# Scan stage of a hybrid decoder step: the sample states advanced once ahead of the 32 steps, and the rotation products made by cosine and by sine over both parts at a time

## The reference

```
bu_re, bu_im = einsum(u, bb_re), einsum(u, bb_im)
h(l) = a * h(l-1) + bu(l)          # complex, a = mag * (cos + i sin), over the 256 prompt tokens from zero
h    = a * h0 + bu                 # for the 8 sample rows: one step from a carried state h0
y    = einsum(c_re, h_re) - einsum(c_im, h_im) + d * u
```

## Time and profile before

| | |
|---|---|
| median of 3 runs | 1678.98 us (1677.73 to 1684.87) |
| the profiled execution | 1680.68 us, its span 1678.9 us |
| PE busy | 1550.0 us (92%) |
| DVE busy | 735.7 us (44%) |
| ACT busy | 330.2 us (20%) |
| POOL busy | 215.4 us (13%) |
| mean granted clock of TensorE | 0.964 |

### The profile page before, as it was taken

How to read it: one execution, slowest core, us unless ns; L and a number is a source line. 1 busy time by engine, 2 the same in 40 slices (tenths; PEclk the granted TensorE clock), 3 DMA queues, 4 the chain that set the end, 5 groups by cost and what they waited for, 6 DMA issues and landing times. The chain is left out here.

```text
span 1678.9 us, 21005 instructions
## 1 busy us (share of the span) xinstructions
PE 1550.0 (92%) x8121; PEld 1093.6 (65%) x8121; DVE 735.7 (44%) x1989; ACT 330.2 (20%) x873; POOL 215.4 (13%) x304
## 2 busy tenths in 40 slices
PE   7999998998989888999999799859999999999996
PEld 5888886776767666888887378735454454455444
DVE  3546429999974743000334300151343343343344
ACT  3111010111113222110112100133123222222214
POOL 1111026656630000110000000120000000000000
PEclk9999998999999889999999899969999999999998
DMA  9743443333342547444576876305999999999971
GB/s 277 225 149 110 151 151 104 106 118 125 99 135 87 158 138 256 151 150 135 175 258 231 299 211 247 153 2 217 404 405 383 404 402 389 394 403 401 382 323 52
DMA packets 203393, 376.19 MB, mean 224 GB/s; under 512 B 25011, under 2 KB 158431, under 8 KB 178450
## 3 DMA queue, kind: packets, MB, share of 16 engines
q1 hardware_dynamic: 198634, 370.62, 60.5%
q10 hardware_dynamic: 4664, 4.28, 0.7%
HBM read 363.44 MB, written 11.54 MB: 223 GB/s over the span
## 5 line engine op out<-in xcount | busy, mean ns | idle before, releaser
L932 PE MATMUL ps<-ring,M 128*128 128x256 f32 x1024 | 246.1, 399 | 1.6 <-ACT M L945 1.6
L932 PEld LDWEIGHTS ps<-ring,M 128*128 128x128 f32 x1024 | 201.1, 200 | 42.3 <-issue 14.6
L2463 PE MATMUL ps<-ring,M 128*64 128x512 f32 x1024 | 223.3, 594 | 0.3 <-ACT M L2552 0.3
L645 PE MATMUL ps<-X,ring 128*128 128x264 f32 x896 | 205.1, 390 | 0.0
L645 PEld LDWEIGHTS ps<-X,ring 128*128 128x128 f32 x896 | 171.0, 192 | 29.2 <-issue 0.4
L2463 PEld LDWEIGHTS ps<-ring,M 128*64 128x64 f32 x1024 | 72.1, 137 | 137.8 <-issue 137.0
L315 PE MATMUL ps<-SH,ring 128*128 128x264 f32 x512 | 116.1, 391 | 6.4 <-PEq L1512 6.4
L1861 PE MATMUL ps<-X,ring 128*128 128x264 f32 x512 | 117.7, 387 | 1.6 <-PEq L1565 1.6
L315 PE MATMUL ps<-X,ring 128*128 128x264 f32 x512 | 114.2, 387 | 1.0 <-PEq L1687 1.0
L2507 PE MATMUL ps<-SH,M 128*64 128x512 f32 x512 | 113.4, 595 | 1.3 <-DVE XT L2680 1.3
L315 PEld LDWEIGHTS ps<-SH,ring 128*128 128x128 f32 x512 | 98.7, 193 | 23.8 <-issue 6.8
(11 more groups left out here) (462 smaller groups left out, 1842.8 us busy)
## 6 DMA issues: line engine op xcount, KB each, us to landing
SH<-in_moe_w_down SPq DMA_DIRECT2D x32, 2048.0 KB, 12.0
ring<-in_moe_w_gate SPq DMA_DIRECT2D x64, 1024.0 KB, 11.6
ring<-in_moe_w_up SPq DMA_DIRECT2D x64, 1024.0 KB, 13.8
ring<-in_w_in SPq DMA_DIRECT2D x14, 2048.0 KB, 8.2
ring<-in_xa_wk SPq DMA_DIRECT2D x8, 2048.0 KB, 9.3
ring<-in_xa_wv SPq DMA_DIRECT2D x8, 2048.0 KB, 9.1
ring<-in_w_out SPq DMA_DIRECT2D x8, 2048.0 KB, 8.6
ring<-in_xa_wq SPq DMA_DIRECT2D x8, 2048.0 KB, 8.6
```

Source lines behind the costliest of these rows:

```text
L645: mm = nc.tensor.matmul(ps[:, n % 4, 0:T], w[:, d, o * P:(o + 1) * P], xn[:, d, :], start=(d == 0), stop=(d == KB - 1))
L932: mm = nc.tensor.matmul(ps[:, kv_bank(s), a * 256:(a + 1) * 256], memT[:, k, a * P:(a + 1) * P], w[:, k, :], start=(k == 0), stop=(k == KB ...
L2463: mm = nc.tensor.matmul(ps[64 * e:64 * e + 64, 0, :], xg[:, p % 3, k, e, :], gate_up_unit(e, half)[:, :, k % 8, :], start=(k == 0), stop=( ...
```

## The change

DVE's program of the scan stage is changed, nothing else. Ahead of the step loop four instructions compute the carried states times `a` for all 32 steps at once, into `carried` (and a helper `carried_b`) in a free part of `work`. In a step one instruction then adds the input to `carried` in place of four that computed the product and the sum. The products with the cosine are made over the real and imaginary parts in one instruction of 128x512 (the cosine repeated by a stride of zero), and those with the sine likewise, ahead of the scans and behind them. The sums and differences stay as they were, and read other places of `pr`.

```diff
+        carried, carried_b = (work[:, 2112 + 512 * i:2624 + 512 * i].rearrange("p (i b t) -> p i b t", i=2, b=TS)
+                              for i in range(2))
...
+                by_cos, by_sin = pr[:, 0:2], pr[:, 2:4]
+                every_b = lambda j, n: s5p[:, j, :].unsqueeze(1).to_broadcast([P, n, 32])
+                both = lambda x: x.rearrange("p i b t -> p (i b) t")
+                tt(both(carried), both(s5h[:, :, :, :]), every_b(AR, 16), ALU.mult)
+                tt(carried_b[:, 0], s5h[:, 1], every_b(NAI, 8), ALU.mult)
+                st(tt(carried_b[:, 1], s5h[:, 0], every_b(AI, 8), ALU.mult))
+                st(tt(both(carried), both(carried), both(carried_b), ALU.add))
                 for t in range(NT):
...
-                    tt(pr[:, 0], br[:, 0:TP], cos, ALU.mult)
-                    tt(pr[:, 1], bi[:, 0:TP], sin, ALU.mult)
-                    tt(pr[:, 2], bi[:, 0:TP], cos, ALU.mult)
-                    stt(hr[:, TP:T], s5h[:, 0, :, t], sc(AR), br[:, TP:T], ALU.mult, ALU.add)
-                    stt(hi[:, TP:T], s5h[:, 1, :, t], sc(AR), bi[:, TP:T], ALU.mult, ALU.add)
-                    tt(pr[:, 3], br[:, 0:TP], sin, ALU.mult).then_inc(bu_taken.sem, bu_taken.up())
+                    tt(by_cos, bu[:, :, 0:TP], cos, ALU.mult)
+                    tt(by_sin, bu[:, :, 0:TP], sin, ALU.mult)
+                    tt(hb[:, t % 4, :, TP:T], carried[:, :, :, t], bu[:, :, TP:T], ALU.add).then_inc(
+                        bu_taken.sem, bu_taken.up())
                     dve.wait_ge(bu_taken.sem, bu_taken.at(t + 1))
-                    tt(gin[:, 0], pr[:, 0], pr[:, 1], ALU.add)
-                    stt(hr[:, TP:T], s5h[:, 1, :, t], sc(NAI), hr[:, TP:T], ALU.mult, ALU.add)
-                    stt(hi[:, TP:T], s5h[:, 0, :, t], sc(AI), hi[:, TP:T], ALU.mult, ALU.add)
-                    st(tt(gin[:, 1], pr[:, 2], pr[:, 3], ALU.subtract))
+                    tt(gin[:, 0], by_cos[:, 0], by_sin[:, 1], ALU.add)
+                    st(tt(gin[:, 1], by_cos[:, 1], by_sin[:, 0], ALU.subtract))
...
-                    tt(pr[:, 0], gsc[:, 0], cos, ALU.mult)
-                    tt(pr[:, 1], gsc[:, 1], sin, ALU.mult)
-                    tt(pr[:, 2], gsc[:, 1], cos, ALU.mult)
-                    tt(pr[:, 3], gsc[:, 0], sin, ALU.mult).then_inc(rot_used.sem, rot_used.up())
+                    tt(by_cos, gsc, cos, ALU.mult)
+                    tt(by_sin, gsc, sin, ALU.mult).then_inc(rot_used.sem, rot_used.up())
                     dve.wait_ge(rot_used.sem, rot_used.at(t + 1))
-                    tt(hr[:, 0:TP], pr[:, 0], pr[:, 1], ALU.subtract)
-                    tt(hi[:, 0:TP], pr[:, 2], pr[:, 3], ALU.add).then_inc(state_ready.sem, state_ready.up())
+                    tt(hr[:, 0:TP], by_cos[:, 0], by_sin[:, 1], ALU.subtract)
+                    tt(hi[:, 0:TP], by_cos[:, 1], by_sin[:, 0], ALU.add).then_inc(state_ready.sem, state_ready.up())
```

More of the change, by code:

```diff
@@ L1052, in _ @@
                 tt, stt = v.tensor_tensor, v.scalar_tensor_tensor
+                by_cos, by_sin = pr[:, 0:2], pr[:, 2:4]
[5 more added lines that the diff above has]
+                st(tt(both(carried), both(carried), both(carried_b), ALU.add))
                 for t in range(NT):
                     q, p = t // 4, t // 2
-                    br, bi = (ps[:, 3 + 2 * (t % 2) + i, :] for i in range(2))
-                    cos, sin = W[:, t % 2, 0, :], W[:, t % 2, 1, :]
+                    bu = ps[:, 3 + 2 * (t % 2):5 + 2 * (t % 2), :]
+                    cos, sin = (W[:, t % 2, i, :].unsqueeze(1).to_broadcast([P, 2, TP]) for i in range(2))
                     sc = lambda j: s5p[:, j, t:t + 1]
```

## The result

| | before | after |
|---|---|---|
| median of 5 runs each | 1678.98 us | 1665.6 us (1662.69 to 1666.87) |
| ratio after / before, 95% interval | | 0.9915 (0.9892 to 0.9937) |
| span of the profiled execution | 1678.9 us | 1663.7 us |
| DVE busy | 735.7 us | 720.2 us |

The change made the kernel 0.85% faster, 1 us from the time forecast. By the medians it is 13.4 us. By the spans of the two profiled executions it is 15.2 us, since the one before stood 1.7 us above its median and the one after stands on it.

A forecast was written before the change was run, and what follows sets the result against it. DVE was taken to bound the scan stage. Savings of 14.6 + 0.65 - 0.9 = 14.4 us from 1680.68 gave 1666.3, and a median of 1664.6 us; range for 8 in 10: 1657 to 1672.

The forecast's parts named there:

- The pitches: DVE's start-to-start distances in a scan step: 0.26, 0.28 and 0.15 us saved, 5.83 us in place of 6.5 without turns.
- The turns with POOL: Two-SBUF-operand DVE instructions and POOL operations block each other in a scan step: 1.25 to 1.35 us, before 1.19.
- its first rival: DVE's new order meets one more POOL operation a step, another 0.4 us: 1676 us, no change; chance 0.10.
- Stretch 14.6 us shorter: PE's second to last input group, 28 steps: 202.3 us in place of 216.9, at 7.14 us a step.
- the one for L1093: L1093, in six steps of the stretch, costs 0.40 us each on DVE, added in full.
- the give-back: Before, a step with L1093 gave part of its cost back by pushing DVE out of POOL's way; none counted after.
- 0.9 lost and 0.65 gained ahead of the stretch: Scan stage's start: four new instructions hold up POOL's first table, 0.9 us lost; first step saves 0.65 us.
- Behind the stretch neither gain nor loss: After PE's last input group PE ends the stage, some 24.5 us, so the saving neither grows nor goes.
- the turns eat the gain: Rival: one more wait for POOL a scan step takes 11 us of the 14: 1676 us; chance 0.10.
- PE takes over: Rival: most turns fall away and DVE's two scan steps fall under PE's 13.1 us: 1650 us; chance 0.11.
- The wide products: Rival: in the scan steps they cost more than two narrow ones, at half speed 1722 us; chance 0.04.
- given back later: Rival: the scan stage gets shorter but a later load isn't ready and takes the time back: 1679 us; chance 0.03.

The follow-up runs named there:

- e3: Changed kernel with POOL's tables left out from step 2 on, so steps reuse the tables of steps 0 and 1: 1649.9 us, one run.
- e7: Kernel before the change with POOL's tables left out from step 2 on, so steps reuse the tables of steps 0 and 1: 1650.85 us, one run.
- e1: Kernel before plus only the four instructions ahead of the loop and one small addition a step, products as before: 1670.72 us against 1681.13, ratio 0.9935.
- e2: Kernel before with only the wide products, the sample rows' four small instructions a step kept: 1672.44 us, ratio 0.9955.
- e4: Changed kernel without the four instructions ahead of the loop, adding the state itself in place of the carried states: 1663.73 us, one run.
- e6: Changed kernel with PE's input groups one chunk later, odd steps' bank release behind the scans, and the scans' factor in PSUM: 1649.65 us, ratio 0.9818.

## Why the prediction was right, point by point

- *DVE bounds the stage, before and after.* Shown: PE waits for DVE 14 times after the change, and 14.3 us lie between its groups (300.82, 315.16, 329.50). e3 and e7 show the floor that PE sets, 13.3 a pair; the forecast read 12.9 without and 13.4 with transposes.
- *The pitches: 0.26 at the inputs, 0.28 at the sum and difference, 0.15 behind the scans.* Shown by e3 and e7, which have no turns: 6.51 and 5.78, 0.73 apart against 0.69; and each part by itself in e1 (0.41, forecast 0.38) and e2 (0.28, forecast 0.28). The unknown, two PSUM banks and a repeated operand, took the nearest row's price: 0.69 us.
- *The turns with POOL would land on the difference, the first scan and the last sum, 1.25 to 1.35 us.* Shown: 1.37, of which 0.12 on the sum was not foreseen. The forecast let the sum start free at 1.46 into the step, but POOL's fourth operation (L1046, 300.34 to 301.07, 0.95 to 1.68 into the step) still runs there; that makes a fourth waiting instruction in the step, which the prediction named as the sign of its first rival, but its wait is less than a third of the 0.4 given there. The forecast had POOL's fifth operation take its turn behind the sum, and it does (301.14).
- *Stretch 14.6 us shorter.* It was 16.2: the term mis-sized is the one for L1093. I added 0.40 in full for each of the six steps with it and counted none of the give-back in the new kernel; the steps' starts at 299.39, 306.55, 313.73, 321.03 and 328.07 show four of them at 28.68, where four times 7.16 is 28.64. So 0.36 comes back each time, 2.2 us in all, less 0.6 for a step of 7.16 in place of 7.14. The prediction's reason for the give-back, that L1093 pushes DVE out of POOL's way, is the smaller part of it. L1093 (L1096 in the changed kernel) fills the time in which DVE otherwise waits at the head of a step, so that the next product starts 1.17 behind the last sum, and not 1.03 (305.52 to 306.55); the sum then starts near the end of POOL's fourth operation and takes 0.43 in place of 0.54:

```profile
319.86 0.85 DVE L1093 TENSOR_TENSOR work<-X 128x256 f32<-128x256 f32 x1
320.63 0.48 DVE L1096 SCALAR_TENSOR_TENSOR SH<-SH,par,ps 128x264 f32<-128x264 f32 x1
321.03 0.68 DVE L1077 TENSOR_TENSOR X<-ps,X 128x512 f32<-128x512 f32 x1
...
322.43 0.43 DVE L1082 TENSOR_TENSOR X<-X 128x256 f32<-128x256 f32 x1
```

- *0.9 lost and 0.65 gained ahead of the stretch.* Its start moved by 0.21 (257.58 to 257.79), and e4 puts the loss alone at 0.86. Here it was read off the trace that an instruction under another engine's wait can still cost, through that engine.
- *Behind the stretch neither gain nor loss.* Wrong by 1.7: the two chunks behind the last input group ran at the low clock. PE's own time counts there, so it was lost. The length of the idle time ahead doesn't explain it: 1.39 to 1.41 stood ahead of four earlier groups too (343.82, 401.13, 429.80, 444.13), and 1.91 ahead of the last group in the kernel before, and the chunks behind all of them ran at full clock. What tells these apart was not tried. The blocks behind gave 0.85 back (1179.3 us from L1020 to the end, 1180.2 before).

The sum: 16.2 - 0.2 - 1.7 + 0.9 = 15.2 us by the spans, against 14.4 forecast. Two errors of the same size stood on either side, 1.6 in the stretch and 1.7 behind it, so that the sum came this close is in part luck.

Of the rivals, the one in which the turns eat the gain is settled: they rose by 0.18 us a step, a quarter of the 0.73 that the pitches save, not by 0.4. The one in which PE takes over is what e3 made true, and e6 came near it. The wide products were not dearer. What the stage gained was not given back later.

The Trainium skill (SBUF — State Buffer, "Who interferes with whom") says that a DVE instruction with two SBUF inputs contends with a GpSimd instruction that reads SBUF, and one with at most one SBUF input, outside the two-port modes, does not. e6 agrees: the same scan, beside the same POOL operation, waited 0.41 us with its factor in SBUF and not at all with it in PSUM (691 ns in the median, 692 at most).

## What to carry to other kernels

Price a fused instruction by start-to-start distances of rows of the same length, and then walk the other engine's operations past the new order by hand: where VectorE and GpSimd both work out of SBUF, each wait that seems to belong to a removed instruction may move to its neighbour (e1). Look for the operand that can leave SBUF: one column in PSUM was worth nearly as much as seven fewer instructions a step (0.42 against 0.56 us). And ask how far the next engine lets the time fall; here PE's floor stood 1 us a pair of steps below (13.3 against 14.3), and the second gain (13.5) used up most of it.

## What the runs showed of the hardware

- A factor repeated with a stride of zero out of one PSUM column serves a scan at full pace: 691 ns for 256 tokens, as the least with SBUF (691).
- Turns go by instruction: between two DVE instructions that stand back to back, POOL gets in. In the steps shown no instruction waited for more than one POOL operation, and the waits were 0.12 to 0.42 us, less than the 0.62 or 0.73 that a POOL operation takes alone.
- With PE's waits for DVE down from 24.4 to 19.2 us, the granted clock of the stretch was 0.99 in place of 0.93, and the same matmuls took 12.5 us less. That the shorter idle times raised the clock was not tried by itself. The stretch went by DVE's steps all the same (28 x 7.16 = 200.5 of 200.67 us).
